# End of an encoder layer: the final gain spread by TensorE, tile 1's rows added by GpSimd, the last tile in column halves

## What is computed

```python
x = x + token_mixer(rms_norm(x, norm_mix), ...)            # attention and gated linear attention
hn = rms_norm(x, norm_ffn)
x = x + hier_moe(hn, router..., expert_w_gate, expert_w_up, expert_w_down)   # each token: 2 of 32 experts
return rms_norm(x, norm_final)

def rms_norm(x, g):
    return x * rsqrt(mean(x * x, axis=-1) + EPS) * g
```

## Time and profile before

| what | value |
|---|---|
| time, median of 3 runs | 604.0 us (603.17 to 604.3) |
| profiled execution, first to last instruction (span) | 601.3 us |
| profiled execution, its own whole time | not given beside the profile; the median of the runs lies 2.7 us above its span |
| PE busy | 576.4 us (96%) |
| DVE busy | 262.7 us (44%) |
| ACT busy | 216.4 us (36%) |
| POOL busy | 60.5 us (10%) |
| DMA | 155.78 MB, mean 259 GB/s |

### The profile page before, as it was taken

How to read it: one execution, slowest core, us unless ns; L and a number is a source line. 1 busy time by engine, 2 the same in 40 slices (tenths; PEclk the granted TensorE clock), 3 DMA queues, 4 the chain that set the end, 5 groups by cost and what they waited for, 6 DMA issues and landing times.

```text
span 601.3 us, 8737 instructions
## 1 busy us (share of the span) xinstructions
PE 576.4 (96%) x3437; PEld 436.4 (73%) x3440; DVE 262.7 (44%) x610; ACT 216.4 (36%) x440; POOL 60.5 (10%) x104
## 2 busy tenths in 40 slices
PE   7999999999999999999999998999999999896896
PEld 4978989888788888888888875666666666553552
DVE  4645677645445766533472386112111211113255
ACT  6644666555786522422252251111111111111114
POOL 3110000001000001100000022021212121112001
PEclk9999999999999999999999999999999999989999
DMA  8365130712231222197789667999999999999995
GB/s 309 80 209 175 59 112 4 289 61 71 71 105 42 65 70 71 36 335 277 289 317 414 257 237 309 384 419 423 423 422 425 423 425 420 424 426 424 423 421 217
DMA packets 59292, 155.78 MB, mean 259 GB/s; under 512 B 8285, under 2 KB 38389, under 8 KB 47601
## 3 DMA queue, kind: packets, MB, share of 16 engines
q1 hardware_dynamic: 54512, 145.74, 63.3%
q0 software_dynamic: 4720, 9.45, 4.1%
q10 hardware_dynamic: 16, 0.00, 0.0%
HBM read 147.31 MB, written 15.75 MB: 271 GB/s over the span
## 4 chain that ended last, share of the span: by engine, by line
PE 85%; DMA 7%; DVE 4%; SPq 1%; ACT 1%; issue 1%; POOL 1%; DVEq 0%; POOLq 0%; ACTq 0%
PE mid_rows L813 17%; PE last_rows L813 16%; PE bank L1271 15%; PE bank L813 7%; PE mid_rows L1291 7%; PE bank L806 6%; DMA slot2b<-expert_w_up 5%; PE bank L1345 2%; PE last_rows L871 2%; PE mid_rows L948 2%; SPq L555 1%; PE mid_rows L1364 1%; PE bank L1371 1%; DMA w<-w_in 1%; PE mid_rows L871 1%
## 5 line engine op out<-in xcount | busy, mean ns | idle before, releaser
L1271 PE MATMUL bank<-slots,xgT 128*64 128x256 f32 x544 | 74.7, 384 | 3.9 <-DMA slot2b<-expert_w_up 2.2
L1944 DVE TENSOR_TENSOR w_low<-w,w_high 128x1024 fp32r<-128x1024 f32 x32 | 39.2, 1225 | 78.6 <-ACT w_high L1548 78.6
L1271 PEld LDWEIGHTS bank<-slots,xgT 128*64 128x64 f32 x544 | 49.4, 138 | 22.9 <-issue 4.4
L1548 ACT ACTIVATE w_high<-w 128x1024 fp32r<-128x1024 f32 x32 | 33.7, 1054 | 48.6 <-PE last_rows L813 48.6
L2370 DVE TENSOR_SCALAR y<-mid_rows,slot_weights 128x512 f32<-128x512 f32 x14 | 10.5, 750 | 86.1 <-PE mid_rows L1291 86.1
L1733 ACT ACTIVATE y<-mid_rows,slot_weights 128x512 f32<-128x512 f32 x14 | 9.6, 687 | 81.3 <-PE mid_rows L1291 59.6
L1271 PE MATMUL bank<-slot2b,xgT 128*64 128x256 f32 x208 | 34.6, 390 | 0.0
L1291 PE MATMUL mid_rows<-slots,hT 128*64 128x512 f32 x112 | 29.1, 594 | 1.3 <-issue 1.3
L1727 ACT ACTIVATE h_silu<-bank 128x256 f32<-128x256 f32 x14 | 5.4, 384 | 68.5 <-PE bank L1271 68.5
L813 PE MATMUL mid_rows<-x_high,w_high 128*128 128x512 f32 x72 | 28.6, 398 | 0.0
L813 PE MATMUL mid_rows<-x_high,w_low 128*128 128x512 f32 x72 | 28.1, 390 | 0.0
(11 more groups left out here) (445 smaller groups left out, 1397.3 us busy)
## 6 DMA issues: line engine op xcount, KB each, us to landing
slots<-expert_w_up SPq DMA_DIRECT2D x18, 1024.0 KB, 24.2
slots<-expert_w_gate SPq DMA_DIRECT2D x17, 1024.0 KB, 12.4
slots<-expert_w_down SPq DMA_DIRECT2D x15, 1024.0 KB, 23.8
slot2b<-expert_w_gate SPq DMA_DIRECT2D x9, 1024.0 KB, 17.4
w<-w_in SPq DMA_DIRECT2D x16, 512.0 KB, 3.6
slot2b<-expert_w_up SPq DMA_DIRECT2D x8, 1024.0 KB, 27.9
slot2a<-expert_w_down SPq DMA_DIRECT2D x6, 1024.0 KB, 21.4
w<-w_in SPq DMA_DIRECT2D x7, 840.0 KB, 4.6
```

Source lines behind the costliest of these rows:

```text
L1271: ins = mm(bank[2][e * SLOTS:(e + 1) * SLOTS, m * FE:(m + 1) * FE], xgT[:, c, e * SLOTS:(e + 1) * SLOTS], weights(own, m, e, c * FE, (c + ...
L1548: A(wh2[:, u % 2, :], raw2[:, u % 2, :], ACT.Copy).then_inc(s["hi_done"], 1)
L1944: V.tensor_tensor(wl2[:, u % 2, :], raw2[:, u % 2, :], wh2[:, u % 2, :].bitcast(F32), ALU.subtract).then_inc(s["lo_done"], 1)
```

## The change

It does five things.

1. **Gain.** SP no longer loads `gfin`. Early on it loads `norm_final` as 8 rows of 128 (`final8`, 4 KB, over a constant that is no longer needed). In the last turn of the pair loop (pair 13 of 0 to 13) PE spreads it by 8 products with a repeated unit column (`final_gain`) into banks 0 and 1, and ACT and DVE copy one half each into `gfin`. PE waits for both copies ahead of `last_turn(0)`.
2. **Tile 1.** POOL adds its two rows of `zt` in place (1024 columns), DVE adds the sum to `x2` (`add_row(1, 0)`), and the two `rows_to_tokens` of tile 1 leave PE. DVE's `accumulate(9, ...)` now stands ahead of `accumulate(8, ...)`.
3. **Rows of tile 3** are loaded in two column halves, and PE waits for each.
4. **Sum of squares of tile 3** is taken in column halves on ACT, each as soon as its half is in the bank.
5. **Last multiplication.** DVE multiplies tile 3's halves by the gain (`last_gain`) as soon as the squares of the half are through, ahead of the inverse root. Afterwards DVE multiplies columns 0 to 511 by the root and ACT columns 512 to 1023, and ACT issues the store of its half from its own queue. `final_norm(2)` stands behind both `last_gain`.

The constant that PE multiplies to stay busy (`keep_busy`) is another one, since the old one's neighbour is overwritten; its shape is the same.

```diff
@@ -306,6 +307,7 @@
         gfin = place_at(YA + WSLOT + NT * 2 * D, "gfin", D)[:, :]
+        final8 = K["ones"][0:KC, :]
@@ -584,6 +587,8 @@
             sp.dma_start(gffn, norm_ffn.partition_broadcast(P)).then_inc(s["gain_in"], 16)
+            sp.wait_ge(s["cb_done"], 2)
+            sp.dma_start(final8, norm_final.rearrange("(c p) -> c p", p=P)).then_inc(s["gain_in"], 16)
@@ -661,16 +666,18 @@
                     sp.wait_ge(s["lx_done"], 4)
-                    sp.dma_start(gfin, norm_final.partition_broadcast(P)).then_inc(s["gain_in"], 16)
-                sp.dma_start(zt[:, t], rows.rearrange("(p w) n -> p w n", w=2) if t == 0 else
-                             rows.rearrange("(i p) n -> p i n", i=2)).then_inc(s[f"rows_in{t}"], 16)
+                    for f in range(2):
+                        cols = slice(f * 512, (f + 1) * 512)
+                        sp.dma_start(zt[:, t, :, cols], rows[:, cols].rearrange("(i p) n -> p i n", i=2)
+                                     ).then_inc(s[("rows_in3", "res_in")[f]], 16)
+                else:
+                    sp.dma_start(zt[:, t], rows.rearrange("(p w) n -> p w n", w=2) if t < 2 else
+                                 rows.rearrange("(i p) n -> p i n", i=2)).then_inc(s[f"rows_in{t}"], 16)
...
-            for f in range(2):
-                cols = slice(f * 512, (f + 1) * 512)
-                sp.wait_ge(s["f_last"], NT + f)
-                sp.dma_start(out[(NT - 1) * P:NT * P, cols], x2[:, NT - 1, cols]).then_inc(s["out_done"], 16)
+            sp.wait_ge(s["f_last"], NT)
+            sp.dma_start(out[(NT - 1) * P:NT * P, 0:512], x2[:, NT - 1, 0:512]).then_inc(s["out_done"], 16)
@@ -792,6 +799,8 @@
             pool.sem_inc(s["moe_done"], 1)
+            pool.wait_ge(s["rows_in1"], 32)
+            nc.gpsimd.tensor_tensor(zt[:, 1, 0, :], zt[:, 1, 0, :], zt[:, 1, 1, :], ALU.add).then_inc(s["zeroed"], 1)
@@ -1292,6 +1301,14 @@
 
+            def final_gain():
+                pe.wait_ge(s["gain_in"], 32)
+                pe.wait_ge(s["xgt_outD"], LAST + 1)
+                for c in range(KC):
+                    ins = mm(bank[c // 4][:, (c % 4) * P:(c % 4 + 1) * P], K["ident"][0:KC, c:c + 1].to_broadcast([KC, P]),
+                             final8, start=True, stop=True, skip_group_check=True)
+                ins.then_inc(s["ltab_done"], 1)
+
@@ -1301,6 +1318,8 @@
                     turn_x(n + 1, (n + 1) % 2, (n + 1) // 2 + 1)
+                else:
+                    final_gain()
@@ -1308,6 +1327,7 @@
 
+            pe.wait_ge(s["gain_in"], 34)
@@ -1384,7 +1404,7 @@
             last_down(0)
-            pe.wait_ge(s["ltab_done"], NT)
+            pe.wait_ge(s["ltab_done"], NT + 1)
@@ -1401,25 +1421,24 @@
             last_down(1)
-            pe.wait_ge(s["ltab_done"], 2 * NT + 1)
+            pe.wait_ge(s["ltab_done"], 2 * NT + 2)
             to_tokens(1, 0, 0, 2, True).then_inc(s["comb_done"], 1)
-            to_tokens(1, 0, 1, 3, True)
+            to_tokens(1, 0, 1, 3, True).then_inc(s["comb_done"], 1)
...
-            pe.wait_ge(s["rows_in1"], 32)
-            rows_to_tokens(1, 0, 3).then_inc(s["comb_done"], 1)
             pe.wait_ge(s["f_acc"], 6)
             to_tokens(1, 1, 0, 1, True).then_inc(s["comb_done"], 1)
-            to_tokens(1, 1, 1, 0, True)
+            to_tokens(1, 1, 1, 0, True).then_inc(s["comb_done"], 1)
             to_tokens(1, 1, 3, 7, False)
-            rows_to_tokens(1, 1, 0).then_inc(s["comb_done"], 1)
             pe.wait_ge(s["mid_in"], 2)
             to_tokens(1, 1, 2, 5, False)
-            for tt, banks in ((2, (4, 5)), (3, (6, 7))):
-                pe.wait_ge(s[f"rows_in{tt}"], 32)
-                for f in range(2):
-                    rows_to_tokens(tt, f, banks[f]).then_inc(s["comb_done"], 1)
+            for tt, f, at in ((2, 0, 4), (2, 1, 5), (3, 0, 6), (3, 1, 7)):
+                if (tt, f) == (3, 1):
+                    pe.wait_ge(s["res_in"], 16 * (NT + 1))
+                elif f == 0:
+                    pe.wait_ge(s[f"rows_in{tt}"], 32)
+                rows_to_tokens(tt, f, at).then_inc(s["comb_done"], 1)
@@ -1746,6 +1765,9 @@
 
+            act.wait_ge(s["ltab_done"], 1)
+            A(gfin[:, 0:512], bank[0][:, :], ACT.Copy).then_inc(s["gain_in"], 1)
+
@@ -1787,15 +1809,29 @@
                 A(mid_rows[:, f * 512:(f + 1) * 512], x2[:, 2, f * 512:(f + 1) * 512], ACT.Copy).then_inc(s["mid_in"], 1)
-            for t in range(NT):
+            for t in range(NT - 1):
                 if t < 2:
-                    act.wait_ge(s["f_acc"], 9 + t)
+                    act.wait_ge(s["f_acc"], (8, 10)[t])
                 else:
-                    act.wait_ge(s["comb_done"], (12, 14)[t - 2])
+                    act.wait_ge(s["comb_done"], 12)
...
+            act.wait_ge(s["ssA_done"], 3 * NT - 1)
+            for f in range(2):
+                act.wait_ge(s["comb_done"], 13 + f)
+                cols = slice(f * 512, (f + 1) * 512)
+                last_squares[f] = step(A(junk3[:, cols], last_rows[:, cols], ACT.Square, accum_out=last_ss[:, f:f + 1]))
+                act.wait_ge(s["act_step"], last_squares[f])
+                if f == 0:
+                    act.wait_ge(s["act_step"], step(A(last_ss[:, 0:1], last_ss[:, 0:1], ACT.Copy, scale=1.0 / D, bias=EPS)))
+            A(rstd3[:, NT - 1:NT], last_ss[:, 1:2], ACT.Identity, scale=1.0 / D, bias=last_ss[:, 0:1]).then_inc(s["ssA_done"], 1)
+            act.wait_ge(s["rstd_done"], 4 * NT)
+            act.wait_ge(s["f_acc"], 12)
+            A(x2[:, NT - 1, 512:D], x2[:, NT - 1, 512:D], ACT.Copy, scale=rstd3[:, NT - 1:NT]).then_inc(s["act_step"], 1)
+            act.wait_ge(s["act_step"], steps[0] + 1)
+            act.dma_start(out[(NT - 1) * P:NT * P, 512:D], x2[:, NT - 1, 512:D]).then_inc(s["out_done"], 16)
@@ -2407,6 +2443,8 @@
                 dve_body(n, (n + 1) % 2, (n + 1) // 2 if n >= 1 else None, following=(n < LAST - 1))
+            dve.wait_ge(s["ltab_done"], 1)
+            V.tensor_copy(gfin[:, 512:D], bank[1][:, :]).then_inc(s["gain_in"], 1)
@@ -2475,30 +2513,43 @@
 
-            def add_row(i):
-                return step(V.tensor_tensor(x2[:, 0, :], x2[:, 0, :], zt[:, 0, i, :], ALU.add))
+            def add_row(t, i):
+                return step(V.tensor_tensor(x2[:, t, :], x2[:, t, :], zt[:, t, i, :], ALU.add))
...
-                for cols in ([slice(0, D)] if t < NT - 1 else [slice(0, 512), slice(512, D)]):
-                    V.scalar_tensor_tensor(out=x2[:, t, cols], in0=summed_rows(t)[:, cols], scalar=rstd3[:, t:t + 1],
-                                           in1=gfin[:, cols], op0=ALU.mult, op1=ALU.mult).then_inc(s["f_last"], 1)
+                V.scalar_tensor_tensor(out=x2[:, t, :], in0=summed_rows(t), scalar=rstd3[:, t:t + 1], in1=gfin,
+                                       op0=ALU.mult, op1=ALU.mult).then_inc(s["f_last"], 1)
+
+            def last_gain(f):
+                cols = slice(f * 512, (f + 1) * 512)
+                dve.wait_ge(s["act_step"], last_squares[f])
+                V.tensor_tensor(x2[:, NT - 1, cols], last_rows[:, cols], gfin[:, cols], ALU.mult).then_inc(s["f_acc"], 1)
...
-            first_row = add_row(0)
+            first_row = add_row(0, 0)
             last_low(1, 0)
             dve.wait_ge(s["dve_step"], first_row)
-            second_row = add_row(1)
+            second_row = add_row(0, 1)
...
+            dve.wait_ge(s["zeroed"], 10)
+            third_row = add_row(1, 0)
+            accumulate(9, 0, 1, 1)
+            dve.wait_ge(s["dve_step"], third_row)
             accumulate(8, 1, 0, 3)
-            accumulate(9, 0, 1, 1)
             accumulate(10, 1, 1, 0)
-            dve.wait_ge(s["gain_in"], 32)
-            for t in range(NT):
-                final_norm(t)
+            dve.wait_ge(s["gain_in"], 34)
+            final_norm(0)
+            final_norm(1)
+            last_gain(0)
+            last_gain(1)
+            final_norm(2)
+            dve.wait_ge(s["rstd_done"], 4 * NT)
+            dve.wait_ge(s["f_acc"], 12)
+            V.tensor_scalar(x2[:, NT - 1, 0:512], x2[:, NT - 1, 0:512], rstd3[:, NT - 1:NT], None, ALU.mult).then_inc(s["f_last"], 1)
```

6 lines of the change are left out of this document (4 added, 2 removed).

## The result

The changed kernel takes **616.75 us** (median of four runs, 615.81 to 618.04). The kernel before took 604.04 us beside it (603.17 to 604.3). The ratio is 1.0216, 95% interval [1.0203, 1.0228]: slower by 12.7 us, where 1.0 us was forecast and 606.6 us was the upper end of the range. The profiled execution took 615.81 us, and its span is 614.0 us against 601.3.

The account below looks back on a forecast made before the run. The weights' stream sets the pace to 560.7 us, then PE alone to 593.7, then ACT, POOL, DVE and stores. Gain 0 plus tail 1.05 on 604.0 gives 605.0 us, range 602.9 to 606.6.

Parts of the forecast that it names:

- The gain by PE (part 1): costed at nothing.: Behind the pair loop: eight products, 1.85 us on PE, hidden by idle time and the wait for up weights; cost 0.
- `last_turn(0)` begins there: After DVE's copy of the gain: PE starts last_turn(0) at 554.35 instead of 551.86, 2.5 us late.
- The cover: Ahead of the up weights at 560.72: gate products end at 560.0, leaving 0.7 us of slack.
- a rival: Cover ahead of 560.72 fails, or POOL takes three passes: 1 us or more on top, 606.0 to 606.8; chance 0.10.
- Tile 1 on POOL: Tile 1's rows: POOL's addition takes 2.15 us, two passes at its cast's rate; ACT begins tile 0 0.5 us later.
- DVE is first: Lock near 585.2: DVE's addition holds to 586.44, POOL adds until 588.6; the forecast's case, 605.0 us, chance 0.36.
- POOL is first: Rival at 585.2: POOL holds DVE up, ACT begins tile 0 at about 591.4, 0.9 us more: 605.9; chance 0.24.
- The norms in a row: ACT's tail: 1.43 us a tile, 0.95 for tile 3's left half; right half's squares through at 596.45.
- the last multiplications: DVE's tail: final_norm(2) waits for the second last_gain, so tile 2's store of 512 KB leaves 1.4 us later.
- the last MB: Final stores: 1 MB starts at 598.1 + 0.75, takes 2.65 us, ends at 601.5; span 602.35, +1.05 us.
- PE's two us at tile 2: PE has tile 2 ready at 591.7 instead of 593.73, unused because ACT reaches tile 2 only at 593.35.
- the sum for parts 2 to 5: Kernel's tail: span goes from 601.3 to 602.35, +1.05 us.

Follow-up runs that it names:

- e7: Changed kernel with PE's wait for the gain's copies moved behind the conditional block and last_ss in dead columns of row_norms, so no buffer moves: 606.41 us.
- e8: e7 with final_norm(2) placed between last_gain(0) and last_gain(1): 606.24 us, +2.4 us against the kernel before.
- e12: Changed kernel, its wait and buffer shift kept, with PE's register load and conditional block taken out: 607.92 us, +4.1 us against the kernel before.
- e6: Kernel before with parts 2 to 5 only (gain by DMA), last_ss in an existing buffer so that no address moves: 605.76 us, +1.9 us.
- e9: e6 with POOL's addition of tile 1's rows held until DVE's second addition of tile 0 is done: 604.84 us, +1.0 us against the kernel before.
- e2: Kernel before with only the eight products added on PE in the pair loop's last turn, no copies, no wait behind: 604.51 us, +1.0 us.
- e11: Kernel before with part 2 alone, POOL held as in e9, DVE's last accumulation of tile 0 ahead of the waiting addition: 603.11 us, -0.7 us.

## Why the prediction was wrong, step by step

**"The gain by PE (part 1): costed at nothing."** This is the step that failed. The products were sized well: 1.85 us forecast, 2.05 measured. So was their chain: y, then the copy, then the turn 2.5 us late (2.64 in e7). What failed is "`last_turn(0)` begins there": PE is ready for it at 557.88, begins at 559.20 and stops again from 559.68 to 564.85. In e7, with the wait behind the jump, it does begin as forecast, at 554.50 against 554.35. I costed the wait by who is queued behind it, and looked only at the next products. Between them and the wait stand a register load and a jump, which the profile doesn't count as busy, and which cost nothing in the kernel before because PE could pass them while the down products of pair 13 were still running; the block of code moved from 552.68 to 553.56, under the turning products and the wait for the gate weights. With the wait ahead of it, the jump is passed only at 557.88, and the fetch lies bare: 1.32 and 5.17 us. The Trainium skill (Runtime: NRT & Kernel Launch, "Instruction fetch mechanics") states the mechanism: code is fetched ahead only in sequence, in 16 KiB blocks, and a taken branch whose target isn't among those at hand has to wait for a DMA. The traces agree, with blocks of 16 KB, with a stop that ends 1.4 to 1.6 us behind the block, and with stops that go when the branch goes. The prediction had no rival of this kind, and so no long tail. Why 4.4 us pass between the jump and the block, among the packets of the weights or elsewhere, is not shown.

**The cover** of 0.7 us ahead of the up weights went with the stop, and a rival named its loss, by another mechanism. I gave it "1 us or more"; it was 7. The cover itself was not too short for the products: e7 and e8 turn on time and lose the cover to the stop of 1.1 us inside the turn. Their gate products begin at 557.68 and 557.87; less that stop it would be 556.6 to 556.8, and the end at about 560.4 (an estimate from the 3.67 us of the earlier trace rows), still ahead of 560.72. Behind the long stop the lower clock adds to it: 9.61 us for gate and up against 7.13 in e12 is 2.5 us.

**What was not a step at all**: the buffer of 8 bytes. I read `last_ss = sb(...)` as free, since it gives no engine any work. It moved every address behind it, and cost 3 us over a stream that sets the pace for some 200 us.

**Tile 1 on POOL.** POOL's addition: 2.15 forecast, 2.35 to 2.40 measured. The estimate of 2.25 by the page of the Trainium skill that the prediction names was nearer than mine by two passes at the cast's rate. Who comes first: I gave "DVE is first" 0.36 and "POOL is first" 0.24. In e6 POOL was first by 0.11 us, and that rival's mechanism and price came out: it forecast 0.9 us for it, and e6 less e9 is 0.9 (ACT begins tile 0 at 591.91 against 590.80); it forecast 605.9 us in all, and e6 measured 605.76. e9 imposes the forecast's own order and gives +1.0 against the forecast's +1.05. In the changed kernel itself the question didn't arise, as said above.

**The norms in a row, the last multiplications, the last MB.** Right in kind, and within 0.4 us in size. ACT took 1.48 us from tile 0 to tile 1 (1.43 forecast) and 0.95 for a half (0.95). `final_norm(2)` began behind the second `last_gain`, and its store went with those of tile 3; nothing moved from 609 to 610 us, and then the MB went at 414 and 381 GB/s, as the earlier trace rows had it at 407. So PE's two us at tile 2 were worth nothing, as forecast. From the start of ACT's first squares to the end of the span the changed kernel takes 12.4 us (601.59 to 614.0) against 11.3 before (589.99 to 601.3); the forecast had 11.85, and e9 has 12.0 (590.80 to 602.8). In e9 ACT begins 0.3 us later than forecast, and the right half's squares are through at 596.78 against 596.45.

In short: the sum for parts 2 to 5 held (+1.0 in e9 against +1.05), its terms within 0.4 us, and two things outside the arithmetic of engines, a jump and an address, made 10 of the 12.7 us.

## What to carry to other kernels

Before putting a wait on an engine, look what its sequencer has to do between that wait and the next real instruction: a jump there was hidden as long as the engine ran ahead of its data, and cost 4 to 7 us once it could not. Put the wait behind the jump, and then see in the trace how much work the engine has at hand until the code behind the jump arrives, 6.65 to 7.1 us later here: products added ahead of that point take some of this work away (e2, e7). In a kernel bound by a stream of transfers, a new small buffer goes behind the large ones or into an existing one, and the address of the large ones is compared before and after. Where two engines that share a lock become ready at the same moment, order them by a semaphore (0.9 us here) instead of hoping for the cheaper order.

No version here beats the kernel before by more than can be measured. The nearest, e11, is 0.7 us faster, with an interval that ends at 1.0000. It lets ACT start tile 0 at 589.46 instead of 589.99 and PE start tile 2's rows at 589.99 instead of 591.77, but tile 1 is summed no earlier: its addition waits for POOL until 589.70, and ACT comes to it at 592.27 instead of 591.94 and so to tile 2 at 593.75, as before. DVE's last norm begins at 597.25 instead of 597.48.
